# Level products of the RWKV inverse with 32 strided moving columns instead of 64, and their results packed in half a PSUM bank

## The reference

```python
strict = jnp.tril(jnp.ones((RW_CHUNK, RW_CHUNK), bool), -1)
...
L_ab = pair(a_dec, b_inv, strict)
...
lhs = jnp.eye(RW_CHUNK, dtype=f32) - L_ab
W1 = lax.linalg.triangular_solve(lhs, a_dec, left_side=True, lower=True, unit_diagonal=True)
U0 = lax.linalg.triangular_solve(lhs, jnp.einsum('bnhts,bnhsv->bnhtv', L_ak, v),
                                 left_side=True, lower=True, unit_diagonal=True)
```

## Time and profile before

| | |
|---|---|
| median of 3 runs | 3291.22 us (3290.09 to 3291.44) |
| the profiled execution's own time | 3291.27 us |
| its span | 3289.4 us |
| mean granted TensorE clock | 0.971 |
| busy: PE / PEld / DVE / ACT / POOL | 3076.6 / 2506.5 / 1615.6 / 554.3 / 2102.4 us |
| matmul records | 19506 |

### The profile page before, as it was taken

One profiled execution on the slowest core, in us unless ns is written; L12 is line 12 of the kernel. 1 busy time (PEld: TensorE's weight loads), 2 busy tenths in 40 slices (PEclk: granted clock), 3 DMA queues, 4 the chain that ended last, 5 costly groups with the idle time before them and its releaser, 6 DMA issues. The chain is left out here.

```text
span 3289.4 us, 45155 instructions
## 1 busy us (share of the span) xinstructions
PE 3076.6 (94%) x19506; PEld 2506.5 (76%) x19506; DVE 1615.6 (49%) x1841; ACT 554.3 (17%) x829; POOL 2102.4 (64%) x941
## 2 busy tenths in 40 slices
PE   8999999889889999999899999998899899999996
PEld 6888777667768778888688887767677678788875
DVE  5331323776646674221883215238766476733127
ACT  1000025333310010000110000453333100100000
POOL 7887675322228778887788877743221488788774
PEclk9999999989999999999999999999899999999998
DMA  4333331111013333322223323311110133333231
GB/s 136 97 97 96 99 111 54 49 43 31 28 34 96 116 96 103 96 96 94 92 90 96 98 95 109 95 48 45 43 35 28 46 90 122 99 100 96 96 103 64
DMA packets 202289, 268.26 MB, mean 82 GB/s; under 512 B 12376, under 2 KB 130476, under 8 KB 201964
## 3 DMA queue, kind: packets, MB, share of 16 engines
q1 hardware_dynamic: 193920, 242.59, 24.3%
q10 hardware_dynamic: 8172, 22.79, 2.0%
HBM read 259.04 MB, written 6.29 MB: 81 GB/s over the span
## 5 line engine op out<-in xcount | busy, mean ns | idle before, releaser
L1069 POOL TENSOR_TENSOR w_hi<-w_raw,zero 128x1024 fp32r<-128x1024 f32 (+2 forms) x468 | 944.6, 2018 | 1111.8 <-PE ps L818 1101.6
L1072 POOL TENSOR_TENSOR w_lo<-w_raw,w_hi 128x1024 fp32r<-128x1024 f32 (+2 forms) x468 | 1159.8, 2478 | 36.7
L818 PE MATMUL ps<-hT_hi,w_hi 128*128 128x512 f32 x2288 | 918.8, 402 | 18.4 <-DVE hT_lo L1491 12.5
L818 PE MATMUL ps<-hT_lo,w_hi 128*128 128x512 f32 x2288 | 898.0, 392 | 0.0
L818 PE MATMUL ps<-hT_hi,w_lo 128*128 128x512 f32 x2288 | 897.1, 392 | 0.0
L818 PEld LDWEIGHTS ps<-hT_hi,w_hi 128*128 128x128 f32 x2288 | 432.4, 189 | 122.4 <-issue 18.7
L818 PEld LDWEIGHTS ps<-hT_hi,w_lo 128*128 128x128 f32 x2288 | 432.3, 189 | 93.2
L818 PEld LDWEIGHTS ps<-hT_lo,w_hi 128*128 128x128 f32 x2288 | 432.8, 189 | 88.9 <-issue 2.9
L1534 DVE TENSOR_TENSOR act_raw<-silu,ps 128x512 f32<-128x512 f32 x88 | 59.9, 681 | 549.6 <-PE ps L818 549.6
L818 PE MATMUL ps<-w_hi,aT_hi 128*128 128x512 f32 x704 | 278.4, 396 | 0.0
L818 PE MATMUL ps<-w_hi,aT_lo 128*128 128x512 f32 x704 | 278.1, 395 | 0.0
(11 more groups left out here) (298 smaller groups left out, 3689.4 us busy)
## 6 DMA issues: line engine op xcount, KB each, us to landing
w_raw<-in_w_in SPq DMA_DIRECT2D x104, 512.0 KB, 3.6
w_raw<-in_ffn_wg SPq DMA_DIRECT2D x176, 256.0 KB, 2.8
w_raw<-in_ffn_wu SPq DMA_DIRECT2D x176, 256.0 KB, 3.1
w_raw<-in_ffn_wd SPq DMA_DIRECT2D x88, 512.0 KB, 3.6
w_raw<-in_w_in SPq DMA_DIRECT2D x96, 128.0 KB, 2.3
w_raw<-in_w_out SPq DMA_DIRECT2D x16, 512.0 KB, 3.7
w_raw<-in_ple_gate SPq DMA_DIRECT2D x16, 512.0 KB, 3.6
ln_rows<-in_ln_g ACTq DMA_DIRECT2D x8, 512.0 KB, 3.9
```

Source lines behind the costliest of these rows:

```text
L818: ins = nc.tensor.matmul(o, l_, r_, start=first, stop=last)
L1069: nc.gpsimd.tensor_tensor(w_split[0][:, q, :, 0:w], w_raw[:, r, :, 0:w], zero[:, 0:1].unsqueeze(2).to_broadcast([P, 2, w]), ALU.add).then_ ...
L1072: nc.gpsimd.tensor_tensor(w_split[1][:, q, :, 0:w], w_raw[:, r, :, 0:w], w_split[0][:, q, :, 0:w].bitcast(F32), ALU.subtract).then_inc(*st ...
```

## The change

The three products of levels 1 to 5 move only the 32 columns of a unit that VectorE reads: the early ones at lines 389 and 401, the late ones at line 407. The moving operand is a strided view (`half_cols`: runs of h words, h = 2 to 32, with gaps of h words between them), and the 32 result columns are packed, unit after unit, in the first 256 of the bank's 512 columns. VectorE's three operations read the packed half (`bank_half`) in place of the strided halves of the whole bank. Level 0 stays as it is. The stationary operands, the number of matmuls and of vector operations, the waits, and the order on every engine stay the same.

```diff
--- before.py
+++ after.py
@@ -303,6 +303,13 @@
         def bank_units(b):
             return b[:, :].rearrange("p (u n) -> p u n", n=HEAD)
 
+        def half_cols(x, height, which):
+
+            return x.rearrange("p (n two s) -> p n two s", two=2, s=height)[:, :, which, :]
+
+        def bank_half(b, height):
+            return b[:, 0:2 * NT * HEAD // 2].rearrange("p (u n s) -> p u n s", u=2 * NT, s=height)
+
         def of_tiles(x, height, which):
 
             return x.rearrange("p t (n two s) -> p t n two s", two=2, s=height)[:, :, :, which, :]
@@ -360,6 +367,15 @@
             def unit_cols(hd, t):
                 return slice(HEAD * (NT * hd + t), HEAD * (NT * hd + t) + HEAD)
 
+            def half_unit_cols(hd, t):
+                return slice(HEAD // 2 * (NT * hd + t), HEAD // 2 * (NT * hd + t + 1))
+
+            def product(b, lev, hd, t, cp, w, x, which):
+
+                h = RX_LEVELS[lev]
+                return nc.tensor.matmul(b[unit(cp), half_unit_cols(hd, t)].rearrange("p (n s) -> p n s", s=h), w,
+                                        half_cols(x[unit(cp), NT * hd + t, :], h, which), start=True, stop=True)
+
             def token_major(i, src):
                 b = take(("rwt", L, ft, i), ("rw_tok", L, ft, i))
                 for t in range(NT):
@@ -386,9 +402,11 @@
                     pe.wait_ge(*after("rw_inv", L, ft, lev - 1))
                 for hd, t in UNITS:
                     for cp in range(2):
-                        ins = nc.tensor.matmul(b[unit(cp), unit_cols(hd, t)], bm[unit(cp), hd, t, 0, :],
-                                               ident()[unit(cp), unit(cp)] if lev == 0 else inv[unit(cp), NT * hd + t, :],
-                                               start=True, stop=True)
+                        if lev == 0:
+                            ins = nc.tensor.matmul(b[unit(cp), unit_cols(hd, t)], bm[unit(cp), hd, t, 0, :],
+                                                   ident()[unit(cp), unit(cp)], start=True, stop=True)
+                        else:
+                            ins = product(b, lev, hd, t, cp, bm[unit(cp), hd, t, 0, :], inv, 0)
                 ins.then_inc(*step("rwx_done", L, ft, lev))
 
             def widen(lev):
@@ -398,14 +416,12 @@
                     b = take(("rwi", L, ft, lev), ("rw_inv", L, ft, lev))
                     for hd, t in UNITS:
                         for cp in range(2):
-                            ins = nc.tensor.matmul(b[unit(cp), unit_cols(hd, t)], invT[unit(cp), NT * hd + t, :],
-                                                   xl[unit(cp), NT * hd + t, :], start=True, stop=True)
+                            ins = product(b, lev, hd, t, cp, invT[unit(cp), NT * hd + t, :], xl, 0)
                     ins.then_inc(*step("rwi_done", L, ft, lev))
                 b = take(("rwj", L, ft, lev), ("rw_invT", L, ft, lev))
                 for hd, t in UNITS:
                     for cp in range(2):
-                        ins = nc.tensor.matmul(b[unit(cp), unit_cols(hd, t)], xl[unit(cp), NT * hd + t, :],
-                                               invT[unit(cp), NT * hd + t, :], start=True, stop=True)
+                        ins = product(b, lev, hd, t, cp, xl[unit(cp), NT * hd + t, :], invT, 1)
                 ins.then_inc(*step("rwj_done", L, ft, lev))
 
             pe.wait_ge(*after("rkv_mix", L, ft, 2))
@@ -662,7 +678,7 @@
                 v.memset(late if lev == 1 else late[:, :, :, 0:hgt // 2], 0.0)
                 now("rwx_done", L, ft, lev)
                 mask = mask64(R64_PAIR + lev).rearrange("p (n two s) -> p n two s", two=2, s=hgt)[:, :, 0, :]
-                v.tensor_tensor(of_units(xl[:, :, :], hgt, 0), of_units(bank_units(bank("rwx", L, ft, lev)), hgt, 0),
+                v.tensor_tensor(of_units(xl[:, :, :], hgt, 0), bank_half(bank("rwx", L, ft, lev), hgt),
                                 mask.unsqueeze(1).to_broadcast([P, 2 * NT, HEAD // (2 * hgt), hgt]), ALU.mult).then_inc(
                     *step("rw_x", L, ft, lev))
 
@@ -695,12 +711,12 @@
                     now("rwi_done", L, ft, lev)
                     now("rw_inv", L, ft, lev - 1)
                     early = of_units(inv[:, :, :], hgt, 0)
-                    v.tensor_tensor(early, early, of_units(bank_units(bank("rwi", L, ft, lev)), hgt, 0), ALU.add).then_inc(
+                    v.tensor_tensor(early, early, bank_half(bank("rwi", L, ft, lev), hgt), ALU.add).then_inc(
                         *step("rw_inv", L, ft, lev))
                 now("rwj_done", L, ft, lev)
                 now("rw_invT", L, ft, lev - 1)
                 late = of_units(invT[:, :, :], hgt, 1)
-                v.tensor_tensor(late, late, of_units(bank_units(bank("rwj", L, ft, lev)), hgt, 1), ALU.add).then_inc(
+                v.tensor_tensor(late, late, bank_half(bank("rwj", L, ft, lev), hgt), ALU.add).then_inc(
                     *step("rw_invT", L, ft, lev))
                 aside(2)
             aside(1)
```

## The result

The changed kernel takes 3303.44 us, the median of 7 runs (3299.05 to 3304.63), against 3290.63 us of 7 runs before (3288.77 to 3291.44). The ratio is 1.0038, with a 95% interval of 1.0028 to 1.0047. So it is slower, by about 0.4%; 3291.0 was forecast, with a range that ended at 3297.5. Two of all the executions in this document, one of e4_low_full (10676.58 us) and one of the kernel before beside e10_after_both (7783.93 us), were slow from end to end for a reason that nothing here shows, and are left out.

What follows compares the result with a forecast made beforehand. PE was taken to bound the kernel, its level products paced by weight loads. From the profiled 3291.27 us, 0 for the spacing and -0.3 for tails and small waits gave 3291.0 us, range 3284.5 to 3297.5 us.

Steps and rivals of the forecast that it cites:

- Term (1): Level products: the 64-column load (58 ns) outlasts the stream (54, then 27 ns), so record spacing stays; 0 us.
- The first rival: Level products: the stream is what costs, records fall towards 14.2 ns, 45 us faster, 3246 us; chance 0.06 for this version.
- small version: Level products: the record falls only to line 375's 26.6 ns, giving 3285.5 us; chance 0.08.
- Term (2): Batch ends: the last record ends 0.025 us sooner, counting only where PE later waits; -0.3 us with the small waits.
- (3): VectorE reads the half bank as one run with the same elements; 0 us, at most under 1 us from `inv` waits.
- (4): Batches in front of the four `inv` waits: cheaper records would buy nothing there; 12 of 112 batches are covered.
- the price of the halved columns for the clock: RWKV cores: none in the sum; the forecast allowed up to four falls of the clock, 6.4 us, within its range.
- the second rival: Level batches, likeliest at `inv` waits: the clock falls more often, 1.6 us a fall; five or more, chance 0.10.

Runs made afterwards that it cites:

- e4_low_full: The changed kernel with levels 1 to 3 moving 64 columns again and only levels 4 and 5 moving 32; 3290.16 us, ratio 1.0000.
- e10_after_both: The changed kernel with one projection block moved from level 2 to before level 1's widen, another before level 5's `inv` wait (first two head pairs); 3286.10 us.
- e8_w32: The changed kernel with only 32 stationary columns loaded in levels 1 to 5 and VectorE's three operations not reading the banks; 3261.35 us, one run.
- e9_two: The changed kernel with only 2 moving columns in levels 1 to 5 and VectorE's three operations not reading the banks; 3358.3 us, one run.
- e3: The changed kernel with levels 4 and 5 moving 64 columns again and only levels 1 to 3 moving 32; 3303.17 us, ratio 1.0042.
- e5: The changed kernel with one block of three 512-column projection matmuls moved from level 2 to before level 1's widen, in every head pair; 3291.98 us.
- e7: The kernel before, with one projection block moved in front of level 5's wait for `inv` in the first two head pairs; 3283.74 us, ratio 0.9982.

## Why the prediction was wrong

**Term (1), the spacing: right.** 0.93 us a batch with 32 columns, 0.93 to 0.96 with 2, 0.50 with half the load. The inference from products of 2 and of 128 columns on 128-wide weights carried over to 64x64 corners. The first rival (the stream costs) is refuted, its small version too: at 26.6 ns a record a batch would have come every 0.85 us.

**Term (2), the tail: mis-sized, without weight.** It gave a record 25 ns less. One line's instructions in the changed kernel (ns min/median/max):

```profile
L376 PE MATMUL ps<-inv,bm x64: 211/219/240, 790.5 to 796.2; 64*64 64x32 f32 x64
```

219 ns, as before, where 192 to 194 was expected: between 64 and 32 moving columns the length doesn't change, so nothing was there for the -0.3 us. It isn't set by the load alone either: in e8_w32 (32 stationary, 32 moving columns) it is 193 ns, and in e9_two (64 stationary, 2 moving) 194:

```profile
L375 PE MATMUL ps<-xl,invT x32: 194/194/215, 744.2 to 745.1; 64*64 64x2 f32 x32
```

What sets it stays open.

**Terms (3) and (4)** held as far as they can be seen: VectorE's operations last 419, 420 and 384 ns, and the four `inv` waits are 4.9 us.

**The step that failed is the price of the halved columns for the clock.** The sum has 0 us for them, the forecast allowed up to four falls, and the second rival, which had the mechanism, got a chance of 0.10. Its price for a fall was fair: 1.6 us for 3.4 is 0.47 us per us, and 0.34 to 0.39 came out. What it had wrong is the place and the length. It called the four `inv` waits, where PE is idle, the likeliest places, named the runs of three level batches only besides, and said against a fall that "PE stays at work through those places". It took a busy PE as safe. The largest loss came in such a run of three batches, at levels 1 and 2, where the products of 2 columns stand ahead, after PE was busy 3.26 of 3.4 us. e3 (levels 1 to 3 halved, the whole loss) and e4 (levels 4 and 5 halved, no loss in ten runs) show it, and e5 takes the loss back with a block moved to that place. And it priced all falls at 3.4 us and took five to be needed, while one stay of 17.1 us is as long as five. The 37.6 us more at half clock are as long as 11 short falls, against the four that the forecast and its range allowed.

What the rows before could have told: a busy PE in a level was one record after another waiting for its load, at 54 ns of stream in 57. Halving the columns therefore halved what the array does in each, and the term counted this as costless because nothing became later.

## What to carry to other kernels

On the products here, whose moving side is no longer than their stationary side, the load sets the pace: a batch took 0.93 to 0.96 us with 64, 32 and 2 moving columns and 0.50 us with half the stationary ones. Fewer moving columns alone save nothing there. Unneeded columns can be what stands between a kernel and a fall to 1.2 GHz: before taking them out, look for stretches in which thin products stand together without a wide one between them. Moving a wide block there took back 11 us in e5, though why isn't shown. A busy PE in the profile is no sign that such a stretch is safe. And a block moved in front of a known wait of PE was worth 6 us (e7), where the whole change was forecast to give 0.3; its own share and the clock's are not separated.

## What was not expected of the hardware

The granted clock fell to 1.2 GHz right behind 3.4 us in which PE was busy 3.39 us (at 856.3 in the change), and it stayed there through stretches in which PE's records leave no gap: 17.1 us of 17.1 in the change, 44.4 of 44.4 with 2 moving columns. A matmul record's length stayed at 218 to 219 ns from 64 to 32 moving columns; it was 193 ns with 32 stationary and 32 moving columns and 194 ns with 64 stationary and 2 moving ones. Products of 32 by 32 on these corners run at 16 ns a record, under the 26.6 ns of line 375, so that was no issue limit.
